# Two narrow projections of a decoder trunk, moved from chunks of their own into wide chunks as guest units

## What is computed

```python
EVEN_SPLITS = (1024, 1536, 24, 512, 512, 64)          # q, kv, branch gates, cq, ckv, rotary key
q_nsa, kv_nsa, g_nsa, cq, ckv, kr = split(h @ even_w_in, EVEN_SPLITS)
gates = sigmoid(g_nsa + gate_b)                        # used by every sparse head
cq = rmsnorm(cq, q_norm); ckv = rmsnorm(ckv, kv_norm); kr = rope(kr, positions)

FOX_SPLITS = (2048, 2048, 2048, 16, 2048)              # q, k, v, forget gate, output gate
q, k, v, f, og = split(h @ fox_w_in, FOX_SPLITS)
q, k = rmsnorm per head
cum = cumsum(log_sigmoid(f + f_b))                     # over the tokens
logit = q . k * scale + cum[query] - cum[key]
```

## Time and profile before

| | us |
|---|---|
| median of three executions | 2775.75 |
| lowest and highest of them | 2767.36, 2777.0 |
| the profiled execution, whole | 2772.71 |
| its span in the trace | 2770.8 |
| TensorE busy in the span | 2581.2 (93%) |
| DVE busy in the span | 1720.6 (62%) |
| ACT busy in the span | 1020.1 (37%) |

### The profile page before, as it was taken

How to read it: one execution, slowest core, us unless ns; L and a number is a source line. 1 busy time by engine, 2 the same in 40 slices (tenths; PEclk the granted TensorE clock), 3 DMA queues, 4 the chain that set the end, 5 groups by cost and what they waited for, 6 DMA issues and landing times.

```text
span 2770.8 us, 29298 instructions
## 1 busy us (share of the span) xinstructions
PE 2581.2 (93%) x11766; PEld 2066.2 (75%) x11766; DVE 1720.6 (62%) x1398; ACT 1020.1 (37%) x947; POOL 3.2 (0%) x11
## 2 busy tenths in 40 slices
PE   5789877889999999999997999999999999999998
PEld 1368656567787788878876888878778788888886
DVE  6566637485766766676656666677677654445445
ACT  1033213244433333333344444444443333333333
POOL 0000000000000000000000000000000000000000
PEclk8789978699999999999998999999999999999999
DMA  8758645476687778777876888789678755655553
GB/s 316 284 203 283 199 151 211 152 257 214 234 312 281 265 251 304 268 268 250 296 215 142 230 183 214 188 237 316 225 252 297 262 187 182 196 182 196 183 185 118
DMA packets 255001, 636.54 MB, mean 230 GB/s; under 512 B 16858, under 2 KB 28084, under 8 KB 229428
## 3 DMA queue, kind: packets, MB, share of 16 engines
q1 hardware_dynamic: 254180, 629.89, 69.2%
q0 software_dynamic: 720, 5.24, 0.5%
HBM read 633.00 MB, written 2.10 MB: 229 GB/s over the span
## 4 chain that ended last, share of the span: by engine, by line
PE 83%; DVE 9%; DMA 3%; ACT 2%; issue 2%; SPq 1%; DVEq 0%; ACTq 0%
PE PS L909 24%; PE PS L911 24%; PE PS L910 24%; DVE WLO L1427 3%; DMA RAW<-in_ada_w 2%; DVE ACC L1440 1%; ACT WHI L554 1%; PE PS L1100 1%; PE PS L958 1%; PE PS L973 1%; PE PS L1130 1%; PE PS L954 1%; PE PS L1287 1%; PE PS L1331 1%; DMA RAW<-in_mla_w_ukv 1%
## 5 line engine op out<-in xcount | busy, mean ns | idle before, releaser
L909 PE MATMUL PS<-WHI,AHI 128*128 128x512 f32 x2120 | 835.2, 394 | 27.6 <-DVE WLO L1427 11.3
L911 PE MATMUL PS<-WHI,ALO 128*128 128x512 f32 x2120 | 828.2, 391 | 0.0
L910 PE MATMUL PS<-WLO,AHI 128*128 128x512 f32 x2120 | 827.7, 390 | 0.0
L1427 DVE TENSOR_TENSOR WLO<-RAW,WHI 128x2048 fp32r<-128x2048 f32 (+2 forms) x222 | 503.6, 2270 | 392.7 <-ACT WHI L554 392.3
L554 ACT ACTIVATE WHI<-RAW 128x2048 fp32r<-128x2048 f32 (+2 forms) x222 | 421.2, 1898 | 709.4 <-PE PS L911 650.2
L1921 DVE TENSOR_TENSOR WLO<-RAW,WHI 128x2048 fp32r<-128x2048 f32 x176 | 403.4, 2292 | 361.7 <-ACT WHI L788 361.1
L788 ACT ACTIVATE WHI<-RAW 128x2048 fp32r<-128x2048 f32 x176 | 337.4, 1917 | 590.9 <-PE PS L911 571.0
L909 PEld LDWEIGHTS PS<-WHI,AHI 128*128 128x128 f32 x2120 | 400.0, 189 | 114.4 <-issue 26.7
L911 PEld LDWEIGHTS PS<-WHI,ALO 128*128 128x128 f32 x2120 | 399.5, 188 | 84.2
L910 PEld LDWEIGHTS PS<-WLO,AHI 128*128 128x128 f32 x2120 | 399.6, 188 | 81.0 <-issue 0.2
L909 PE MATMUL PS<-WHI,GHI 128*128 128x512 f32 x960 | 382.1, 398 | 16.2 <-DVE GLO L1525 8.4
(11 more groups left out here) (289 smaller groups left out, 1519.3 us busy)
## 6 DMA issues: line engine op xcount, KB each, us to landing
RAW<-in_ffn_w SPq DMA_DIRECT2D x264, 1024.0 KB, 5.2
RAW<-in_ada_w SPq DMA_DIRECT2D x192, 1024.0 KB, 5.6
RAW<-in_fox_w_in SPq DMA_DIRECT2D x64, 1024.0 KB, 8.6
RAW<-in_even_w_in SPq DMA_DIRECT2D x28, 1024.0 KB, 5.3
RAW<-in_even_w_out SPq DMA_DIRECT2D x16, 1024.0 KB, 6.0
RAW<-in_fox_w_out SPq DMA_DIRECT2D x16, 1024.0 KB, 6.3
GROW<-in_ada_b POOLq DMA_DIRECT2D x4, 1024.0 KB, 5.5
RAW<-in_nsa_cmp_w_k SPq DMA_DIRECT2D x4, 1024.0 KB, 6.3
```

The source lines that it names most:

```text
L909: mm(dst(tb), xh, whi[:, k, :], start=first and k == 0, stop=False)
L910: mm(dst(tb), xh, wlo[:, k, :], start=False, stop=False)
L911: ins = mm(dst(tb), xl, whi[:, k, :], start=False, stop=last and k == nk - 1)
L1427: TT(m.w_view(m.WLO, u), m.w_view(m.RAW, u), m.w_view(m.WHI, u).bitcast(F32), ALU.subtract).then_inc(m["lo_ready"].sem, 1)
```

## The change

- `even_in` has seven chunks instead of eight. The 88-column unit becomes a guest of chunk 5: loaded and split behind unit 1, multiplied on TensorE behind unit 1 and the transposes of chunk 4, into PSUM bank 6. DVE copies it (`gk_kept`) behind the low part of unit 2; TensorE transposes it into bank 7 behind unit 3; DVE reads that (`gk_turned`, `KRR`, `gates_in`) in its `between` of unit 3. Chunks 5 and 6 have three `a` units each instead of two.
- `fox` has 12 chunks instead of 13. The 16-column unit becomes a guest of chunk 1, which is now k0, in bank 5. DVE's first two steps stand behind the low part of unit 2, the exponential and the logarithm behind the high part of unit 3, DVE's last one behind the low part of unit 3. The three TensorE steps stand after units 0, 1 and 2 of v0, and DVE's three reads behind the low parts of units 0, 1 and 2 of v0.
- The output gate chunks carry 4, 3, 2, 2 `a` units instead of 3, 2, 3, 2; the accumulator buffers simply alternate, so that q0 and k0 have different ones, where before they had the same.

```diff
-        self.even_in = [plan.chunk("even_in", i, rows(win, 512 * i + (24 if i > 4 else 0), 512), 2) for i in range(7)]
-
-        self.even_in.append(plan.chunk("even_in", 7, [
-            (tuple(win[:, a:b].rearrange("(k p) n -> p k n", p=P) for a, b in ((2560, 2584), (3608, 3672))), KT, 88, 0)], 2))
+        narrow = (tuple(win[:, a:b].rearrange("(k p) n -> p k n", p=P) for a, b in ((2560, 2584), (3608, 3672))), KT, 88, 0)
+        self.even_in = [plan.chunk("even_in", i, rows(win, 512 * i + (24 if i > 4 else 0), 512), 2 + (i > 4), extra=narrow if i == 5 else None)
+                        for i in range(7)]
...
-        self.fox_kind = [("q", 0), ("f", 0), ("k", 0), ("v", 0)] + [(kind, part) for part in (1, 2, 3) for kind in "qkv"]
+        self.fox_kind = [(kind, part) for part in range(4) for kind in "qkv"]
...
-        self.fox_g = [plan.chunk("fox_g", i, rows(fin, 3 * D + 16 + 512 * i, 512), (3, 2, 3, 2)[i], buf=(i + 1) % 2) for i in range(4)]
+        self.fox_g = [plan.chunk("fox_g", i, rows(fin, 3 * D + 16 + 512 * i, 512), (4, 3, 2, 2)[i]) for i in range(4)]
```

In the plan, `Plan.chunk` appends the guest behind unit 1:

```diff
             units.append(self.unit("w", src=src, nk=nk, cols=cols, kt0=kt0))
+            if extra and j == 1:
+                src, nk, cols, kt0 = extra
+                units.append(self.unit("w", src=src, nk=nk, cols=cols, kt0=kt0))
+                units[-1].extra = True
             while done < ada * (j + 1) // len(weights):
```

ACT:

```diff
                 if i:
                     first(chunks[i - 1])
+                if c.extra:
+                    hi(c.extra)
                 prep(c, (2,))
...
+            if c.extra and j == 3:
+                wait("fz_ready", 0)
+                m["f_exp"].tick(A(m.FE, m.FE, ACT.Exp), 0)
+                wait("f_exp", 0)
+                m["f_log"].tick(A(m.FL, m.FE, ACT.Ln, bias=1.0), 0)
```

TensorE:

```diff
                     between(c, j)
+                    if c.extra and j == 1:
+                        turned_unit(c.extra, stat(c, c.extra), m.PS[0:c.extra.cols, 6 if c.key[0] == "even_in" else 5, 0:T])
...
+        def even_between(c, j):
+            if c.extra and j == 3:
+                wait("gk_kept", 0)
+                for tb in range(2):
+                    ins = turn(m.PS[:, 7, P * tb:P * tb + 88], m.GK[:, P * tb:P * tb + P], m.CON[0:88, C_ID:C_ID + 88])
+                m["gk_turned"].tick(ins, 0)
...
-            if c.key == ("fox", m.fox_at["k", 0]) and j == 1:
-                sigmoids_turned()
-            if c.key == ("fox", m.fox_at["k", 0]) and j == 2:
-                cumulate()
-            if c.key == ("fox", m.fox_at["k", 0]) and j == 3:
-                cumulate_turned()
+            if c.key == ("fox", m.fox_at["v", 0]) and j < 3:
+                (sigmoids_turned, cumulate, cumulate_turned)[j]()
```

DVE:

```diff
+        def even_between(c, j):
+            if c.extra and j == 2:
+                dve.wait_ge(m["w_used"].sem, c.extra.n + 1)
+                dve.wait_ge(m["lo_split"].sem, m["lo_split"].value)
+                m["gk_kept"].tick(V.tensor_copy(m.GK, m.PS[0:88, 6, 0:T]), 0)
+            if c.extra and j == 3:
+                wait("gk_turned", 0)
+                gk = m.PS[:, 7, 0:T].rearrange("p (b n) -> p b n", b=2)
+                V.tensor_copy(m.KRR[:], gk[:, :, 24:88])
+                m["gates_in"].tick(TT(m.GATES[:], gk[:, :, 0:24], m.GB[:].unsqueeze(1).to_broadcast([P, 2, 24]), ALU.add), 0)
...
-            if c.key == ("fox", m.fox_at["k", 0]) and j == 2:
+            if c.extra and j == 2:
+                dve.wait_ge(m["w_used"].sem, c.extra.n + 1)
+                link(TS(m.FZ, m.PS[0:16, 5, 0:T], m.FB[0:16, 0:1], None, ALU.add))
+                m["fz_ready"].tick(STT(out=m.FE, in0=m.FZ, scalar=-1.0, in1=m.FZ, op0=ALU.mult, op1=ALU.min), 0)
+            if c.extra and j == 3:
+                wait("f_log", 0)
+                m["ls_ready"].tick(STT(out=m.FZ, in0=m.FZ, scalar=0.0, in1=m.FL, op0=ALU.min, op1=ALU.subtract), 0)
+            if c.key == ("fox", m.fox_at["v", 0]) and j == 0:
                 wait("ls_turned", 0)
...
-            if c.key == ("fox", m.fox_at["k", 0]) and j == 3:
+            if c.key == ("fox", m.fox_at["v", 0]) and j == 1:
                 wait("cum_done", 0)
...
-            if c.key == ("fox", m.fox_at["v", 0]) and j == 0:
+            if c.key == ("fox", m.fox_at["v", 0]) and j == 2:
                 wait("cumt_done", 0)
```

More of the change, by code:

```diff
@@ L71, in __init__ @@
         self.src, self.nk, self.cols, self.kt0 = src, nk, cols, kt0
+        self.extra = False
         if kind == "a":
@@ L79, in __init__ @@
         self.name, self.i, self.units, self.buf, self.before = name, i, units, buf, before
-        self.w = [u for u in units if u.kind == "w"]
+        self.w = [u for u in units if u.kind == "w" and not u.extra]
+        self.extra = next((u for u in units if u.extra), None)
         self.key = (name, i)
@@ L119, in unit, with chunk @@
         return u
-    def chunk(self, name, i, weights, ada=0, buf=None):
+    def chunk(self, name, i, weights, ada=0, buf=None, extra=None):
         units, done = [], 0
@@ L708, in _ @@
         run(m.even_in, even_first, even_second)
+        wait("gates_in", 0)
+        m["gates_ready"].tick(A(m.GATES[:], m.GATES[:], ACT.Sigmoid), 0)
         for i in range(2):
@@ L850, in fox_first @@
             kind, part = m.fox_kind[c.i]
[L851 to L856, removed]
+            if kind == "v":
                 m["heads_kept"].tick(A(m.V_F[:, part], m.acc(c.buf), ACT.Copy), c.key)
@@ L918, in halves, with turned_unit @@
             return pick
-        def turned_product(u, stat, dst, first, last):
+        def turned_unit(u, stat, dst):
+            pe.wait_ge(m["lo_ready"].sem, u.n + 1)
             whi, wlo = (w[:, u.n % 2, 0:u.nk * u.cols].rearrange("p (k n) -> p k n", n=u.cols) for w in (m.WHI, m.WLO))
@@ L924, in turned_product @@
                 xh, xl = stat(k, None)
-                mm(dst, whi[:, k, :], xh, start=first and k == 0, stop=False)
+                mm(dst, whi[:, k, :], xh, start=k == 0, stop=False)
                 mm(dst, wlo[:, k, :], xh, start=False, stop=False)
-                ins = mm(dst, whi[:, k, :], xl, start=False, stop=last and k == u.nk - 1)
-            return ins
+                ins = mm(dst, whi[:, k, :], xl, start=False, stop=k == u.nk - 1)
+            ins.then_inc(m["w_used"].sem, 1)
         def unit(c, j, stat, ready, rows=(0, 1)):
@@ L1113, in even_after @@
         def even_after(c):
-            if c.i < 7:
-                staged(c.key, (0, P) if c.i in (3, 4) else range(0, 512, P))
-        run(m.even_in, lambda c, u: halves(m.AHI, m.ALO, u.kt0), lambda c, j: ("lo_split", ("norm", 0, j)), even_after)
+            staged(c.key, (0, P) if c.i in (3, 4) else range(0, 512, P))
+        def even_between(c, j):
[4 more added lines that the diff above has]
+                m["gk_turned"].tick(ins, 0)
+        run(m.even_in, lambda c, u: halves(m.AHI, m.ALO, u.kt0), lambda c, j: ("lo_split", ("norm", 0, j)), even_after, between=even_between)
         finish((0, G1))
[L1120 to L1123, removed]
         for i, units in enumerate(m.cmp_in):
             wait("cmp_b", i)
-            wait(*m.freed_by(("even_in", 6 + i)))
+            wait(*m.freed_by(("even_in", 6 - i)))
             for u in units:
@@ L1483, in run @@
                     lo(u)
-                    if len(c.w) == 1 and c is not chunks[-1]:
-                        lo(chunks[i + 1].w[0])
+                    if u.extra:
+                        continue
                     seen += 1
@@ L1643, in even_second @@
                 split_lo(c.key, m.CQL[:, at:at + 4, :], m.TF[:], m.CQH[:, at:at + 4, :])
-        run(m.even_in, even_first, even_second)
+        def even_between(c, j):
[8 more added lines that the diff above has]
+                m["gates_in"].tick(TT(m.GATES[:], gk[:, :, 0:24], m.GB[:].unsqueeze(1).to_broadcast([P, 2, 24]), ALU.add), 0)
+        run(m.even_in, even_first, even_second, between=even_between)
         finish((0, G1))
[L1648 to L1651, removed]
         for i in range(2):
```

38 lines of the change are left out of this document (9 added, 29 removed).

## The result

The changed kernel takes 2813.05 us (median of four, 2811.49 to 2820.89) against 2776.38 us: a ratio of 1.0144 with a 95% interval of 1.0114 to 1.0173, slower by 1.4%. Its profiled execution took 2811.49 us with a span of 2809.5, 38.7 us more than the span before. The forecast was 2783 us, made up of 8.3 us more than before, with a range of 2767 to 2793. Further down, one of the six executions of the kernel with the reads moved ran at a granted clock of 0.55 and took 4338.7 us; it is left out, and the figures of that kernel are of the other five.

The account below looks back on a forecast made before the run. TensorE, busy for 93% of the span, was taken as the bound. +3.6 (`even_in`) and +4.7 (`fox`) sum to +8.3 us: 2784 against the median, stated as 2783; 80% range 2767 to 2793, own range 2779 to 2787.

Parts of the forecast that it names:

- The rest: Everything outside the two places: output gate chunks taken as 0 (0 to +5 us), SP waits for nothing new, POOL's queue untouched.
- The end of `even_in`: Last chunks of `even_in` up to the compression: -10.1 tail, +6.0 guest, +5.7 idle, +2.0 clock, in all +3.6 us.
- The gap of 5.7: Before chunk 6 of `even_in`: TensorE idles 5.7 us for the low part queued behind DVE's read of the transposed guest.
- the wait for `ST` of 4.2: After chunk 6's last product in `even_in`: nothing covers the norm, so TensorE idles 4.2 us before its transposes.
- The start of `fox`: From f's old start to the first scores: -9.3 +0.8 +8.0 +0.4 +4.8, in all +4.7 us.
- The three gaps of 2.6, 2.6 and 2.8: In v0 of `fox`: TensorE stands still for DVE's read and one whole low part, three times, +8.0 us.
- The choice of 1.6 us for each: Clock loss behind each of the three gaps in v0: seven matmuls at 0.23 us, +4.8 us (bounds 0 and 8.7).
- The output gate chunks: First output gate chunk with four `a` units instead of three: total unchanged, 0 taken, 0 to +5 us possible.
- The rival of a transfer as the bound: Fourth `a` load in the first output gate chunk, or forget weights in v0: +5 more, 2788 us; chance 0.07.
- The new waits are hidden: Both places: DVE's reads served before TensorE needs the next low part, -12.2 us, 2763.5 us; chance 0.10.
- The clock does not come back: v0, first to third gap: three units at 1.2 GHz, +14.4 instead of +4.8, total +17.9, 2794 us; chance 0.07.
- The gaps come, the clock stays: v0 of `fox`: the three short gaps pass without clock loss, sum +3.5, 2779 us; chance 0.14.

## Why the prediction was wrong

- **The step that failed** is the list of what the change removes, in the part on the two places and in "The rest". The diff also took out the look-ahead to the next chunk's unit for every chunk with a single unit. I read it as part of the narrow chunks that went and gave it no term, which put it at nothing without a reason; it served the eight `mla` chunks as well. The runs put it at 31 us in the kernel before, without any guest, and at 28 us as what comes back when it is restored. None of the rivals covers it either, since none is about `mla`. The mechanism is the very one that the prediction had named for the four new reads (a read that waits for TensorE, with the next low part queued behind it on DVE).
- **The end of `even_in`**: +3.6 forecast, +4.8 in the profile. The gap of 5.7 came as 5.64, the wait for `ST` of 4.2 as 4.23, last product to compression 15.7 against 15.4. Moving the one read gives back 10.2 us by the medians and 7.7 in the profile; gap and clock were put at 7.7.
- **The start of `fox`**: +4.7 forecast, +2.7 in the profile. The three gaps of 2.6, 2.6 and 2.8 came as 2.48, 2.48 and 2.70, the 0.8 ahead of v0 as 0.82; the 0.4 ahead of q1 did not come. Most of the difference was clock. The windows behind the gap ahead of chunk 6 and behind the three gaps, in the changed kernel:

```profile
305.70:310.70 5.00, 4.98 (x14) 3.99 (x15) 4.56 (x10) 0.20 (x1) 0.00 (x0) 0.63 1.04 399
...
1569.80:1574.80 5.00, 4.98 (x22) 4.10 (x23) 3.37 (x8) 2.01 (x2) 0.00 (x0) 1.00 0.72 206
1579.50:1584.50 5.00, 4.97 (x16) 4.05 (x17) 0.00 (x0) 0.00 (x0) 0.00 (x0) 0.69 0.75 191
1589.50:1594.50 5.00, 4.91 (x15) 3.92 (x16) 5.00 (x4) 0.00 (x0) 0.00 (x0) 0.67 0.75 200
```

  Two gaps cost 6 and 7 matmuls' time as in the earlier trace rows, the first none: 3 us instead of 4.8. In the kernel with the look-ahead alone it was again two of three, but the first and the third:

```profile
1533.80:1538.80 5.00, 4.98 (x16) 4.01 (x17) 3.36 (x8) 2.01 (x2) 0.00 (x0) 0.72 0.71 199
1544.80:1549.80 5.00, 4.99 (x22) 4.15 (x23) 0.00 (x0) 0.00 (x0) 0.00 (x0) 1.00 0.75 191
1553.40:1558.40 5.00, 4.93 (x15) 3.92 (x16) 5.00 (x4) 0.00 (x0) 0.00 (x0) 0.66 0.75 199
```

  The choice of 1.6 us for each was right for two in three. Eight matmuls fewer in five us, 1.8, behind the gap ahead of chunk 6 is near the 2.0 taken.
- **The output gate chunks**: put at 0, and the stage from the first scores on is 1189.3 us long against 1189.6. The sign of being wrong that the prediction named, idle TensorE there, did show once: 0.75 us at 1858, ended by a low part, where the kernel before has no gap. The rival of a transfer as the bound got no more than that.
- **The rivals.** "The new waits are hidden" gave 12.2 us less than before; once the look-ahead is back and the reads are moved, the chip shows a gain of that order (14.0 us by the medians, 5.7 when it ran again; the ratios are 0.9955 and 0.9974). It was not how the change was written. "The clock does not come back" didn't happen: behind each of the three gaps the full clock was back within the 5 us of the windows. "The gaps come, the clock stays" holds for one gap in three.
- **The range.** 2767 to 2793 would have held the part that the prediction covered (2785.36 measured with the look-ahead back, 2783 forecast). It didn't hold the whole.
- **The arithmetic.** Three small slips change nothing: 24 x 0.43 is 10.3 and not 10.2, the 2.9 us of clock for the long gap add up to 2.7 from their own parts, and the forecast's own range takes its lower bound from 2784 and its upper one from 2783.

## What to carry to other kernels

When a change deletes a special case in a shared loop, list every caller that met its condition, and not only the ones that the change is about: here two chunks went and the eight of `mla` lost their cover. Where each queue works in the order of its program, let the consumer's wait stand one unit behind the producer's step. In the same unit, the preparation queued behind the wait starts only when the producer has run dry, and here each such place cost at least one whole piece of preparation (2.5 to 10.8 us). A short piece of work removed as overhead may be the cover of something else, as the 88-column product was for the norm of ckv (4.23 us of waiting without it).

## What was not expected of the hardware

The clock's answer to gaps of the same length is not fixed. Of the three gaps of 2.5 to 2.7 us in v0, two were followed by a granted clock of 0.66 to 0.72 over 5 us and one by 1.00, and which one changed between two kernels with the same instructions there. The Trainium skill ("TensorE: Matmul & The Clock Gate", "HAM oscillation — how this bites in real kernels") describes the back and forth of the clock between bursts; the trace agrees that a wait can cost clock on top of itself, and shows in addition that one as short as 2.5 us can, at 1.4 to 1.6 us (6 or 7 matmuls of 0.23 us).
